# Sums of squares for the next norm: other PSUM columns, and a later place in the order of TensorE, in a two-layer hybrid decoder trunk

## The reference, cut to what matters

```python
def rmsnorm(x, g):
    y = x * rsqrt(mean(x * x, axis=-1) + EPS)
    return y * g

x = x + 0.5 * rmsnorm(swiglu(rmsnorm(x, n[0]), w1_gu, w1_down), n[1])
m, S_a, S_r = mixer(rmsnorm(x, n[2]), ...)      # w_in, GLA and retention heads, w_out
x = x + rmsnorm(m, n[3])
x = x + 0.5 * rmsnorm(swiglu(rmsnorm(x, n[4]), w2_gu, w2_down), n[5])
```

## Time and profile before

| | |
|---|---|
| time, median of 3 runs | 2269.41 us (2269.36 to 2269.57) |
| the profiled execution | 2269.25 us |
| its span, from the first instruction to the last | 2267.4 us |
| TensorE busy with matmuls | 2222.5 us, 98% of the span |
| VectorE, ScalarE, GpSimd busy | 842.3, 817.8 and 947.4 us |
| mean granted clock of TensorE | 0.998 of full speed |
| the chain that ended last | 94% TensorE |

### The profile page before, as it was taken

One profiled execution on the slowest core, in us unless ns is written; L12 is line 12 of the kernel. 1 busy time (PEld: TensorE's weight loads), 2 busy tenths in 40 slices (PEclk: granted clock), 3 DMA queues, 4 the chain that ended last, 5 costly groups with the idle time before them and its releaser, 6 DMA issues.

```text
span 2267.4 us, 43365 instructions
## 1 busy us (share of the span) xinstructions
PE 2222.5 (98%) x17639; PEld 2191.9 (97%) x17639; DVE 842.3 (37%) x1166; ACT 817.8 (36%) x1429; POOL 947.4 (42%) x776
## 2 busy tenths in 40 slices
PE   8999999999999999999999999999999999999998
PEld 7999999999989999999999999999999889999998
DVE  5222200589366422220152222006883772222102
ACT  4332333442344433332343333334424443333333
POOL 3444444444214444444444444453442334444442
PEclk9999999999999999999999999999999999999999
DMA  6223223322234232223322322332222333232222
GB/s 173 87 84 92 72 85 89 91 76 74 66 82 131 75 92 84 86 74 90 113 67 84 91 83 73 90 100 73 79 72 58 99 112 93 83 89 85 76 85 76
DMA packets 382588, 197.57 MB, mean 87 GB/s; under 512 B 8868, under 2 KB 381400, under 8 KB 382360
## 3 DMA queue, kind: packets, MB, share of 16 engines
q1 hardware_dynamic: 365680, 186.93, 28.8%
q10 hardware_dynamic: 16808, 9.20, 1.4%
HBM read 186.80 MB, written 9.31 MB: 86 GB/s over the span
## 4 chain that ended last, share of the span: by engine, by line
PE 94%; DVE 4%; ACT 1%; issue 1%; DMA 0%; ACTq 0%; DVEq 0%
PE ps L529 87%; PE ps L692 1%; PE ps L850 1%; DVE x L1439 1%; DVE y L1433 0%; DVE y_out L1433 0%; DVE xs_lo L1377 0%; PE ps L667 0%; PE ps L791 0%; PE ps L764 0%; DVE q_lvl L1524 0%; PE ps L867 0%; PE ps L770 0%; PE ps L797 0%; ACT xs_hi L1026 0%
## 5 line engine op out<-in xcount | busy, mean ns | idle before, releaser
L465 POOL TENSOR_TENSOR w_lo<-raw,w_hi 128x512 fp32r<-128x512 f32 (+1 forms) x728 | 914.7, 1261 | 1219.1 <-ACT w_hi L1053 1219.0
L529 PE MATMUL ps<-xs_hi,w_hi 128*128 128x256 f32 (+1 forms) x3712 | 789.0, 290 | 16.9 <-DVE xs_lo L1377 13.5
L529 PE MATMUL ps<-xs_hi,w_lo 128*128 128x256 f32 (+1 forms) x3712 | 786.4, 289 | 0.0
L529 PE MATMUL ps<-xs_lo,w_hi 128*128 128x256 f32 (+1 forms) x3712 | 783.6, 288 | 0.0
L1053 ACT ACTIVATE w_hi<-raw 128x512 fp32r<-128x512 f32 (+1 forms) x728 | 420.1, 585 | 959.9 <-PE ps L529 959.0
L529 PEld LDWEIGHTS ps<-xs_hi,w_hi 128*128 128x128 f32 x3712 | 604.5, 189 | 25.9 <-DVE xs_lo L1377 10.6
L529 PEld LDWEIGHTS ps<-xs_lo,w_hi 128*128 128x128 f32 x3712 | 604.2, 189 | 0.4
L529 PEld LDWEIGHTS ps<-xs_hi,w_lo 128*128 128x128 f32 x3712 | 600.9, 188 | 0.0
L1398 DVE TENSOR_TENSOR tmp<-ps,rstd_pre 128x544 f32<-128x544 f32 x88 | 63.8, 725 | 641.4 <-PE ps L529 628.4
L529 PE MATMUL ps<-h_hi,w_lo 128*128 128x256 f32 x1272 | 267.2, 289 | 0.0
L529 PE MATMUL ps<-h_lo,w_hi 128*128 128x256 f32 x1272 | 266.1, 288 | 0.0
(11 more groups left out here) (197 smaller groups left out, 1751.9 us busy)
## 6 DMA issues: line engine op xcount, KB each, us to landing
raw<-in_w_gu_dram SPq DMA_DIRECT2D x176, 512.0 KB, 3.8
raw<-in_w_in_dram SPq DMA_DIRECT2D x56, 512.0 KB, 3.8
raw<-in_w_down_dram SPq DMA_DIRECT2D x64, 384.0 KB, 3.4
raw<-in_w_down_dram SPq DMA_DIRECT2D x64, 320.0 KB, 3.1
raw<-in_w_out_dram SPq DMA_DIRECT2D x16, 512.0 KB, 3.9
ret_state<-in_state_ret_dram SPq DMA_DIRECT2D x8, 512.0 KB, 6.0
out_dram<-ret_state ACTq DMA_DIRECT2D x8, 512.0 KB, 5.0
x_tok<-in_x_prompt_dram SPq DMA_DIRECT2D x4, 512.0 KB, 6.5
```

The costliest lines, as they stand in the source:

```text
L465: pool.tensor_tensor(lo, raw[:, u, k0:k0 + n, :], hi.bitcast(F32), ALU.subtract)\
L529: mm = pe.matmul(bank_part(bank, a), w, v[:, kx, TOK[a]], start=(start and n == 0), stop=(stop and n == 2))
```

## The change

The sums of squares are written to three pieces of PSUM that no tile uses: 256 tokens to columns 0 to 255 of bank 0, 224 to columns 288 to 511 of bank 1, and the last 64 to columns 288 to 351 of bank 3. So `pre_stats` has three matmuls in place of two, and ScalarE takes Ln in three instructions, followed by the one Exp as before. Since banks 6 and 7 aren't touched, TensorE's two waits for `pre_log` are gone. And `pre_stats` stands elsewhere: in the feed-forward sub-layers between the two halves of unit 3, in the mixer between the fourth and the fifth block of the gate tile.

```diff
+        ROOM = 512 - (T - TA)
+        STATS_PLACE = ((slice(0, TA), ps[:, 0, 0:TA]), (slice(TA, TA + ROOM), ps[:, 1, T - TA:512]),
+                       (slice(TA + ROOM, T), ps[:, 3, T - TA:T - TA + T - TA - ROOM]))
             def pre_stats(l, q):
                 wait(pe, xsq_step, l, q * KP + KP - 1)
-                for a in range(2):
-                    mm = pe.matmul(bank_part(6, a), ones, x_sq[:, 0, TOK[a]], start=True, stop=True)
+                for cols, place in STATS_PLACE:
+                    mm = pe.matmul(place, ones, x_sq[:, 0, cols], start=True, stop=True)
                 mm.then_inc(pre_sum.sem, 1)
...
                 unit(g0, 2, KD, xs_hi, xs_lo, 0, 4, True, True)
+                unit(g0, 3, KD, xs_hi, xs_lo, 0, 6, True, True, halves=(0,))
                 pre_stats(l, 2 * f)
-                wait(pe, pre_log, l, 2 * f)
-                unit(g0, 3, KD, xs_hi, xs_lo, 0, 6, True, True)
+                unit(g0, 3, KD, xs_hi, xs_lo, 0, 6, True, True, halves=(1,))
...
                 wait(pe, a_split, l, 0)
-                wait(pe, pre_log, l, 1)
                 for k in range(KD):
+                    if k == KD // 2:
+                        pre_stats(l, 1)
...
                 in_tile(l, 3)
-                pre_stats(l, 1)
                 gate_tile(l)
...
                 wait(act, pre_sum, l, q)
-                root(rstd_pre[:, :], pair(3), q, pre_log, pre_ready, l)
+                for cols, place in STATS_PLACE:
+                    o = act.activation(rstd_pre[:, cols], place, ACT.Ln, bias=eps, scale=1.0 / D)
+                o.then_inc(pre_log.sem, 1)
+                wait(act, pre_log, l, q)
+                act.activation(rstd_pre[:, :], rstd_pre[:, :], ACT.Exp, scale=-0.5).then_inc(pre_ready.sem, 1)
```

## The result

The changed kernel takes 2292.15 us (median of 5 runs, 2291.63 to 2293.66), the kernel before 2269.57 us in the same runs: 22.6 us slower, ratio 1.0099, 95% interval 1.0086 to 1.0113. The forecast was 2288.2 us; its range ended at 2292.0. The profiled execution took 2293.66 us, the slowest of the five, with a span of 2291.9 us.

A forecast was written before the change was run, and what follows sets the result against it. The prediction took TensorE's stream plus its holes as the bound: +13.9 us feed-forward delay, -0.3 gate tile and +5.2 clock make +18.8 us, so 2288.2 us, range 2282 to 2292.

The forecast's parts named there:

- What bounds: Whole kernel: TensorE's stream plus its holes; GpSimd waits of 0.7 us in all show the feed-forward chain already late.
- Delay per place, 3.47 us: Four feed-forward sub-layers: group 1 starts 3.47 us later, from moved half unit, three Ln and third matmul; +13.9 us in all.
- three Ln: On ScalarE in the feed-forward chain: 1.06 us in place of one Ln of 0.71 us, +0.35 us.
- the third matmul: In the feed-forward sum: two more records for the same columns, +0.10 us, between nothing and 0.26 us.
- No gain from the removed waits: Feed-forward sub-layers: the removed 0.80 us wait for Ln lies inside the new 4.4 us wait and gives nothing.
- Gate tile, -0.15 us each with a new wait of 0.7: Mixer, two places: a 0.7 us wait for VectorE's tile 1 replaces that for Ln; -0.3 us in all.
- The clock, 1.3 us each, 5.2 us: At four 4.4 us waits ahead of group 1: clock halves for 3.41 us, partly while TensorE waits; +5.2 us.
- the rival that I gave 7%: Four feed-forward waits: the clock stays low longer, another 1.6 us each, 2294.6 us; chance 7%.
- The row that I misread: Earlier trace's two 2.57 us waits: clock falls 3.07 and 3.75 us after the wait began, mean 0.53 over 3.41 us.
- The price of 0.47 us for a microsecond at half speed: Products at half clock: a fall lying wholly on products costs 3.41 x 0.47 = 1.6 us.
- The cited rule: Pauses between tiles re-throttle TensorE's array each time; by it all four feed-forward places fall, giving 2288.2 us.
- The lower of the two rivals of the clock: Four feed-forward waits: same delays but the clock stays full, 2283.0 us; chance 14%.

The follow-up runs named there:

- x4: Changed kernel, with ScalarE splitting both high halves of group 1's unit 0 ahead of Ln in the feed-forward sub-layers: 2267.71 us.
- x7: Changed kernel, with the feed-forward sub-layers' sum another half unit later, behind all of unit 3: 2305.52 us.
- x1: Kernel before, with the sum in three pieces in the new banks and no waits for `pre_log`, but at its old place: 2269.07 us.
- x9: Kernel before, with the change at the gate tile only, feed-forward sub-layers as before: 2269.12 us.
- x3: Changed kernel, with eight ones-matmuls, results unused, in TensorE's wait ahead of group 1: 2282.97 us.
- x8: Changed kernel, with four ones-matmuls, results unused, in TensorE's wait ahead of group 1: 2288.67 us.
- x2: Kernel before, with the change in the feed-forward sub-layers only, mixer as before: 2290.56 us.
- x10: Kernel before, with new banks, feed-forward sum at its old place, early split of group 1's unit 0, gate tile's sum in its middle: 2264.62 us.

## Why the prediction was right and wrong

- *What bounds.* Right. The 0.7 us of waits for GpSimd in the earlier trace rows did say that the chain behind the sum had no slack. x4 and x7 show it from both sides: without the split behind h the wait is 0.3 us, with the sum 3.02 us later it is 3.05 us longer.
- *Delay per place, 3.47 us.* 3.36 measured. The half unit was 3.02, three Ln took 1.02 us where I had 1.06, so 0.30 us more than one and not 0.35, and 0.04 us is left for the third matmul in place of 0.10. 13.4 us against 13.9.
- *No gain from the removed waits.* Right; x1 has them removed alone, and they come back as 1.25 us for GpSimd.
- *Gate tile, -0.15 us each with a new wait of 0.7.* -0.12 and 0.59 us; the trace of x9 has the same 0.59 us and 11.89 us in place of 12.02, which its time (0.5 us less, within the noise) can't confirm.
- *The clock, 1.3 us each, 5.2 us: the step that failed.* It is 2.7, 2.6, 2.4 and 1.5 us, 9.2 us. I took from two waits of 2.57 us that a fall lasts 3.41 us, carried that to waits of 4.3 us, and counted the part of it that passes in the wait as a saving. The runs showed otherwise: the falls that began in the wait lasted longer. In the profile three of the four begin 2.9 to 3.6 us after the wait's start, that is 0.7 to 1.4 us before its end, and last 6.83 us, so 5.5 to 6.1 us of products run at half speed; the fourth begins 0.9 us behind it and lasts 3.41 us. This was the rival that I gave 7%, with this very reason (the first low stretch is partly idle), and against which I had written that both falls seen ended after one stretch. But both of those began behind their waits, and two falls behind shorter waits weren't evidence for longer ones. x3 shows that the term is the clock and nothing else.
- *The row that I misread.* The windows of 3.41 us in the earlier trace rows with a mean of 0.53 begin 0.23 us too late; put right, the mean is 0.50:

```profile
729.53:732.94 3.41, 3.41 (x15) 3.12 (x14) 3.41 (x7) 1.85 (x5) 0.00 (x0) 0.50 0.39 115
1849.10:1852.51 3.41, 3.41 (x14) 2.84 (x13) 3.41 (x8) 1.97 (x5) 0.00 (x0) 0.50 0.20 60
```

So the falls came 2.84 and 3.52 us after the waits began, not 3.07 and 3.75. The price of 0.47 us for a microsecond at half speed is 1 less the mean of 0.53. It came out near what was measured, by luck: 0.46 by the pairs of matmuls (0.46 us in place of 0.25), 0.45 by the stages (1.5 us for 3.41).
- *The cited rule.* The trace bears out what the Trainium skill ("TensorE: Matmul & The Clock Gate", the section on HAM oscillation) says, that a pause between tiles throttles the array and is then paid for: each of the four waits of 4.26 us brought a fall.
- *Sum.* 13.4 - 0.2 + 9.2 = 22.4 us at the places that the forecast named. The forecast was 3.95 us too low. In the terms of the profile the clock was 4.0 us short, the delay 0.5 too high and the gate tile 0.1 short; 0.16 is the kernel before, which now has a median of 2269.57 us, and the last 0.2 us can't be placed. The lower of the two rivals of the clock, that it holds, is out at these places; the four delays alone, as x3 has them, would have come near its 2283.0 us.

What stays open: what decides whether the fall begins in the wait or behind it, or doesn't come at all. x8 has none and one behind 2.0 us, x2 one fall in the wait and three behind it, with the same work around them. And the profile after shows one more fall, in the second mixer, which is 1.1 us longer than the first for it (281.3 against 280.2 us); x2 has one in both, at 281.4 us, x4, x7, x8 and x10 in one. And there is none at the start of the first layer's second feed-forward, where the kernel before has one and where it cost 0.3 us. Neither was followed further.

## What to carry to other kernels

A wait that is removed is a gain only if what stands behind the wait isn't on the path too. Follow the released engine's order to the next thing that the waiting engine needs, and look for a small wait there: here 0.2 us was enough to say that the slack was zero, and every microsecond by which the producer was moved back came out in full. The cure was in the idle time of another engine: 8.8 us of ScalarE ahead of Ln, in which it could have made the weights that came last.

## What the runs showed of the hardware

- A standstill of TensorE cost more than its length. Waits of 4.26 us were followed by 5.5 to 6.1 us of products at half clock in three of four places, 2.4 to 2.7 us of time each, so that a hole of 4.26 us cost 6.7 to 7.0.
- How long the clock stayed low went with where TensorE stood when it fell: falls that began at or behind the end of a wait lasted 3.41 us in all profiles, those that began in a wait of 4.26 us 6.83 us, and in waits of 7.3 us 6.83 or 10.24 us. Each microsecond of products at half clock cost about 0.45 us.
- A wait of 2.57 us was followed by a fall in 18 of 24 places, one of 1.7 us in none.
- Ones-matmuls with unused results in the hole keep the clock: 3.7 us of them in each of the four holes saved 9.2 us in all, with 0.3 us of hole left; with 2.0 us left, three of four places still fell, 1.5 us each.
- The three matmuls into columns of banks that hold finished tiles took 0.95 us of TensorE's stream, and reading them back in three pieces 0.30 us more than in one.
